# Three early loads outside the expert ring, ScalarE's loads moved to SyncE's queue, norm rows spread by matmuls, gates weighed later, last pair's loads in pieces

## The reference, cut to what matters

```python
x = layer_norm(DEEPNORM_ALPHA * x + mix, ln1_g, ln1_b)           # 256 tokens x 1024
logits = x @ router_w + router_b                                 # 32 experts
top_val, top_idx = top_k(logits, 4);  gates = softmax(top_val)
for each expert e and its tokens:
    gt = min(xb @ w_gate[e] + b_gate[e], 7)                      # w_gate, w_up, w_down: 1024 x 1024 f32 each
    up = clip(xb @ w_up[e] + b_up[e], -7, 7)
    ys = (gt * sigmoid(1.702 * gt) * (up + 1)) @ w_down[e] + b_down[e]
ffn[token] += gate * ys
x = layer_norm(DEEPNORM_ALPHA * x + ffn, ln2_g, ln2_b)
```

## Time and profile before

| | us |
|---|---|
| time, median of 3 runs | 2271.95 (2269.96 to 2273.84) |
| the profiled execution's own time | 2273.94 |
| its span, first to last instruction | 2272.1 |
| PE busy | 2092.2 (92%) |
| DVE busy | 837.5 (37%) |
| ACT busy | 583.3 (26%) |
| PE of the expert matmuls (L940) | 691.6 busy, 77.5 idle before them |
| DMA queue q1 (SP) | 589.54 MB |

### The profile page before, as it was taken

The page is one execution under the profiler, slowest core; times in us unless marked ns, Lnnn a source line. Parts: engine busy times, 40 slices in busy tenths (PEclk is TensorE's granted clock), DMA queues, the critical chain, the costliest instruction groups (busy, mean ns, idle before and its releaser), DMA issues.

```text
span 2272.1 us, 27092 instructions
## 1 busy us (share of the span) xinstructions
PE 2092.2 (92%) x11528; PEld 1397.2 (61%) x11528; DVE 837.5 (37%) x1507; ACT 583.3 (26%) x993; POOL 71.8 (3%) x119
## 2 busy tenths in 40 slices
PE   6988999999899988999999979899899999998887
PEld 3766888878687568999988933333334333433333
DVE  4353534352385546765456521111111121111112
ACT  3222423242242545544356310000000000000001
POOL 0000000000000330000031000000000000000000
PEclk8999999999999999999999989999999999999999
DMA  9543334233422554545532779999999999999996
GB/s 361 186 149 111 111 111 148 100 114 102 148 80 77 186 178 145 186 165 179 194 115 87 270 267 428 428 427 427 428 428 427 428 428 426 429 428 427 428 428 272
DMA packets 163040, 593.93 MB, mean 261 GB/s; under 512 B 10945, under 2 KB 83649, under 8 KB 137569
## 3 DMA queue, kind: packets, MB, share of 16 engines
q1 hardware_dynamic: 158848, 589.54, 65.7%
q10 hardware_dynamic: 4064, 2.58, 0.6%
HBM read 591.05 MB, written 1.05 MB: 261 GB/s over the span
## 4 chain that ended last, share of the span: by engine, by line
PE 74%; DMA 16%; DVE 5%; ACT 3%; issue 1%; ACTq 1%; SPq 1%; DVEq 0%
PE ps L940 21%; PE ps L283 14%; PE ps L284 13%; PE ps L285 13%; DMA ring<-in_w_up_dram 12%; DMA ring<-in_ada_w_dram 3%; PE ps L911 2%; PE ps L892 2%; DVE wr L1067 2%; PE ps L405 2%; ACT big L2012 1%; PE ps L419 1%; PE ps L413 1%; PE ps L720 1%; PE ps L965 0%
## 5 line engine op out<-in xcount | busy, mean ns | idle before, releaser
L940 PE MATMUL ps<-ring,big 128*64 128x512 f32 x3072 | 691.6, 606 | 77.5 <-DMA ring<-in_w_up_dram 50.5
L940 PEld LDWEIGHTS ps<-ring,big 128*64 128x64 f32 x3072 | 252.3, 139 | 489.5 <-issue 481.5
L283 PE MATMUL ps<-h_hi,wr 128*128 128x512 f32 (+1 forms) x960 | 341.6, 356 | 29.0 <-DVE h_lo L1119 24.7
L1067 DVE TENSOR_TENSOR wr<-ring,wr 128x1024 fp32r<-128x1024 f32 (+1 forms) x248 | 285.9, 1212 | 136.6 <-ACT wr L1712 136.5
L284 PE MATMUL ps<-h_lo,wr 128*128 128x512 f32 (+1 forms) x960 | 333.4, 347 | 0.0
L285 PE MATMUL ps<-h_hi,wr 128*128 128x512 f32 (+1 forms) x960 | 333.3, 347 | 0.0
L1712 ACT CAST wr<-ring 128x1024 fp32r<-128x1024 f32 (+1 forms) x248 | 238.8, 1033 | 126.3 <-PE ps L285 101.6
L283 PEld LDWEIGHTS ps<-h_hi,wr 128*128 128x128 f32 x960 | 185.4, 193 | 61.2 <-issue 34.4
L284 PEld LDWEIGHTS ps<-h_lo,wr 128*128 128x128 f32 x960 | 185.6, 193 | 23.4 <-issue 2.9
L285 PEld LDWEIGHTS ps<-h_hi,wr 128*128 128x128 f32 x960 | 185.1, 193 | 22.0
L2012 ACT ACTIVATE big<-ps,xT 128x128 f32<-128x128 f32 x64 | 24.1, 456 | 361.7 <-PE ps L892 361.7
(11 more groups left out here) (305 smaller groups left out, 2571.7 us busy)
## 6 DMA issues: line engine op xcount, KB each, us to landing
ring<-in_w_gate_dram SPq DMA_DIRECT2D x64, 2048.0 KB, 22.2
ring<-in_w_up_dram SPq DMA_DIRECT2D x62, 2048.0 KB, 18.4
ring<-in_w_down_dram SPq DMA_DIRECT2D x60, 2048.0 KB, 22.2
ring<-in_ada_w_dram SPq DMA_DIRECT2D x24, 2048.0 KB, 10.8
ring<-in_ffn_w_up_dram SPq DMA_DIRECT2D x44, 1024.0 KB, 7.6
ring<-in_ffn_w_down_dram SPq DMA_DIRECT2D x16, 1408.0 KB, 6.1
ring<-in_w_in_dram SPq DMA_DIRECT2D x9, 2048.0 KB, 8.0
ring<-in_odd_w_qkv_dram SPq DMA_DIRECT2D x6, 2048.0 KB, 8.1
```

What stands on the lines that cost most here:

```text
L283: e.matmul(o, l[0], r[0], start=first, stop=False)
L940: ins = e.matmul(pts[hf][HALF[z], :], lhs[:, k, HALF[z]], wt[:, k % 4, 512 * hf:512 * hf + 512], start=k == 0, stop=False, skip_group_chec ...
L1067: e.tensor_tensor(wr[:, x], ring[:, x], h.bitcast(F32), SUB).then_inc(s_wlo, 1)
```

## The change

- Loads 7, 8 and 9 (the second expert's last half of up, both experts' first half of down, of pair 0) go to twelve free pieces of SBUF outside the ring, in four DMAs each, with semaphores of their own (`EARLY`). 7 and 8 are issued behind load 2, once the merged rows are there; 9 behind load 6. The ring goes on with load 10 in slot 0 (`nth`).
- ACT issues none of the six DMAs. `b_down` and the two rows of the second norm (4 KB each, not spread) are issued by SP behind load 24. The sixteen small loads of `g8b8` are issued by SP one by one between the weight tiles of the second feed-forward part.
- The first norm's gain is spread by a matmul of ones with diagonal matrices, which DVE writes in pairs 2 and 7; the shift, times ALPHA, is added into the open banks in the same way, in place of a row in `GT`. The second norm's rows are spread by four matmuls, at pairs 7, 9, 11 and 13, and copied to SBUF by ACT.
- `select(0)` calls `gathered(0)` before `weigh`; the first pair's gates are turned at the end of pair 0, not before it; ACT's exponentials come behind `gathered(0)`.
- The last pair's gate k 4 to 7 and up k 0 to 3 come in pieces too. `last_scatter` starts with the half that DVE evacuates.

```diff
+    EARLY = {7: (big[:, 9088:10112], big[:, 10112:11136], big[:, 8064:9088], wkf[:, 0:1024]),
+             8: (big[:, 3072:4096], big[:, 4096:5120], big[:, 2048:3072], xT[:, 0:4, L:512]),
+             9: (xT[:, 4:8, L:512], wkf[:, 1024:2048], zz[:, :], big[:, 11136:12160])}
+    def nth(u):
+        return u if u < 7 else u - len(EARLY)
-    PIECES = [(LAST + 6, 0, 2), (LAST + 6, 2, 3), (LAST + 6, 3, 4), (LAST + 8, 0, 2), (LAST + 8, 2, 4),
+    PIECES = [(LAST + 2, 0, 2), (LAST + 2, 2, 4), (LAST + 4, 0, 2), (LAST + 4, 2, 4), (LAST + 6, 0, 2), (LAST + 6, 2, 3), (LAST + 6, 3, 4), (LAST + 8, 0, 2), (LAST + 8, 2, 4),
               (LAST + 10, 0, 2), (LAST + 10, 2, 3), (LAST + 10, 3, 4)]
...
         def last_scatter(b):
-            for n in range(2):
-                e.wait_ge(*emptied(("y", b, n)))
             for q in range(2):
                 for n in range(2):
+                    if q == 0:
+                        e.wait_ge(*emptied(("y", b, n)))
...
             both(pts, HT[turn_of(b)], u + 8, ("y", b, 0), emptied(("ht", b, 1)))
+            if b == 0:
+                turn_gates(0, U[1])
...
             if b in (4, 8):
-                e.wait_ge(s_rowg, 16)
-                e.matmul(pt[:, :], ones[0:1, :], grow[:, 512 * i:512 * i + 512], start=True,
-                         stop=True).then_inc(fullsem(("G", i)))
+                e.wait_ge(s_diag, 8 * i + 4)
+                e.matmul(pt[:, :], ones[:, :], dgG, start=True, stop=True).then_inc(fullsem(("G", i)))
             if b in (6, 10):
+                for n in range(2):
+                    e.matmul(ps[2 * n + i][:, :], ones[:, :], dgB, start=False, stop=False, skip_group_check=True)
...
+            if b in (7, 9, 11, 13):
+                pt = take(e, ("l2", i), bank=7)
+                e.matmul(pt[:, :], ones[0:1, :], l2row[i // 2][:, 512 * (i % 2):512 * (i % 2) + 512], start=True,
+                         stop=True).then_inc(fullsem(("l2", i)))
...
         gather(0, (6, 7))
-        turn_gates(0, 6)
...
             if b == 0:
+                gathered(0)
                 weigh()
...
+            if b in (2, 7):
+                for dg, x, by in ((dgG, "l1g", 1.0), (dgB, "l1b", ALPHA)):
+                    for c in range(4):
+                        e.tensor_scalar(dg[:, P * c:P * c + P], ident, col(x, 4 * i + c), by, MULT, MULT).then_inc(s_diag, 1)
...
-        e.dma_start(bdn[0:NE, :], a["b_down_2"]).then_inc(s_late2[0], 16)
-        e.wait_ge(s_blo, 2)
-        flat = a["cols"].rearrange("p c -> c p")
-        for row, sem_, c in ((grow, s_rowg, COLS["l1g"]), (bdn[NE:NE + 1, :], s_rowb, COLS["l1b"])):
-            e.dma_start(row.rearrange("o (c p) -> o c p", c=KC), flat[c:c + KC, :].unsqueeze(0),
-                        allow_slow_non_contiguous=True).then_inc(sem_, 16)
-        e.dma_start(l2g, a["ln2_2"][0:1, :].to_broadcast([P, D])).then_inc(s_late2[1], 16)
-        e.dma_start(l2b, a["ln2_2"][1:2, :].to_broadcast([P, D])).then_inc(s_late2[2], 16)
...
+            if b in (7, 9, 11, 13):
+                e.wait_ge(*filled(("l2", i)))
+                e.copy((l2g, l2b)[i // 2][:, 512 * (i % 2):512 * (i % 2) + 512], bank(("l2", i))[:, :]).then_inc(freesem(("l2", i)), 1)
...
         for t in range(W_O + 3, NW - 2):
             w(t)
+            i, c = divmod(t - W_O - 5, KC)
+            if 0 <= i < 2:
+                e.dma_start(g8b8[16 * c:16 * c + 16, 8 * i:8 * i + 8], g8[COLS[("l1g", "l1b")[i]] + c],
+                            allow_slow_non_contiguous=True).then_inc(s_g8, 16)
...
+            if u in EARLY:
+                for i, to in enumerate(EARLY[u]):
+                    rows_ = src[z].rearrange("(p k) n -> p k n", k=KC)[:, 4 * hf + i, :]
+                    e.dma_start(to, rows_ if len(to.shape) == 2 else rows_.rearrange("p (a b) -> p a b", b=L)).then_inc(
+                        s_early[u - 7], 16)
+                return
...
         expert(2)
+        e.wait_ge(*filled(("T2", 23)))
+        e.wait_ge(s_mlo, KC)
+        expert(7)
+        expert(8)
         e.wait_ge(*wlast[NW - 2])
         expert(3)
         expert(4)
         e.wait_ge(*wlast[NW - 1])
         expert(5)
         expert(6)
-        for u in range(7, 12 * (NE // 2)):
+        e.wait_ge(s_blo, 2)
+        e.wait_ge(*filled(("lgt", 1)))
+        expert(9)
+        for u in range(10, 12 * (NE // 2)):
             expert(u)
+            if u == 24:
+                e.dma_start(bdn, a["b_down_2"]).then_inc(s_late2[0], 16)
+                for i in range(2):
+                    e.dma_start(l2row[i], a["ln2_2"][i:i + 1, :]).then_inc(s_late2[1 + i], 16)
```

More of the change, by code:

```diff
@@ L174, in build @@
     s_alpha, s_xhat = sem("s_alpha"), sem("s_tail_normed")
-    s_piece = [sem(f"s_last_pair{i}") for i in range(8)]
+    s_piece = [sem(f"s_last_pair{i}") for i in range(12)]
+    s_early = [sem(f"s_early{i}") for i in range(3)]
     def cols_of(w, c0, n):
@@ L342, in landed_expert @@
     def landed_expert(u):
-        return s_w[u % 7], 16 * sum(x not in in_pieces for x in range(u % 7, u + 1, 7))
+        if u in EARLY:
+            return s_early[u - 7], 64
+        return s_w[nth(u) % 7], 16 * sum(x not in in_pieces and x not in EARLY and nth(x) % 7 == nth(u) % 7 for x in range(u + 1))
     def rows_used(kind, u):
@@ L938, in both @@
                     for z in range(2):
[L939 to L943, removed]
+                        if v + z not in EARLY:
+                            wt = view(ring, SLOT * XS[nth(v + z) % 7], 4, D)[:, k % 4, 512 * hf:512 * hf + 512]
+                        elif len(EARLY[v + z][k % 4].shape) == 3:
+                            wt = EARLY[v + z][k % 4][:, 2 * hf:2 * hf + 2, :]
+                        else:
+                            wt = EARLY[v + z][k % 4][:, 512 * hf:512 * hf + 512]
+                        ins = e.matmul(pts[hf][HALF[z], :], lhs[:, k, HALF[z]], wt, start=k == 0, stop=False,
+                                       skip_group_check=True)
+                        if k % 4 == 3 and hf == 1 and v + z not in EARLY:
+                            ins.then_inc(s_wused[nth(v + z) % 7])
                     if k == KC - 1 and hf == 0 and first:
@@ L979, in pair @@
             pts = [take(e, ("y", b, 0), bank=G[0]),
-                   take(e, ("y", b, 1), bank=G[1], by=(s_wused[last % 7], last // 7 + 1))]
+                   take(e, ("y", b, 1), bank=G[1], by=(s_wused[nth(last) % 7], nth(last) // 7 + 1))]
             e.wait_ge(*emptied(("ht", b, 0)))
             both(pts, HT[turn_of(b)], u + 8, ("y", b, 0), emptied(("ht", b, 1)))
+            if b == 0:
+                turn_gates(0, U[1])
             if nxt:
@@ L1612, in dve @@
         chosen(0)
[L1613 to L1615 removed]
+        e.tensor_scalar(alphaI, ident, ALPHA, None, MULT).then_inc(s_alpha, 1)
         for b in range(NE // 2):
@@ L1687, in dve @@
             aggr_at[n] = tail(e.bn_aggr(mv[n], bst[n]))
-        e.wait_ge(s_late2[1], 16)
-        e.wait_ge(s_late2[2], 16)
+        for i in range(4):
+            e.wait_ge(*emptied(("l2", i)))
         for n in range(2):
@@ L2036, in act @@
         gathered(0)
-        gates_turned(0)
+        e.wait_ge(s_gneg, 1)
+        for n in range(2):
+            ins = e.activation(ex4[:, n, :], top[:, n, 0:4], ACT.Exp, bias=top[:, n, 8:9], accum_out=top[:, n, 9:10])
+        ins.then_inc(s_gexp, 1)
         for b in range(NE // 2):
@@ L2215, in sync @@
         w(NW - 2)
-        for i, x in enumerate(("l1g", "l1b")):
-            src = a["cols"].rearrange("(b k) c -> c b k", k=KC)
-            for c in range(KC):
-                e.dma_start(g8b8[16 * c:16 * c + 16, 8 * i:8 * i + 8], src[COLS[x] + c],
-                            allow_slow_non_contiguous=True).then_inc(s_g8, 16)
         e.wait_ge(*emptied(("S2", 23)))
```

48 lines of the change are left out of this document (27 added, 21 removed).

## The result

The changed kernel took 2254.76 us (median of 5, 2254.24 to 2259.89) against 2273.05 for the kernel before (median of 5, 2269.96 to 2273.84): a ratio of 0.993, 95% interval 0.9915 to 0.9945, so 18.3 us faster. The prediction was 2251.8 with a range of 2246 to 2263.

The account below looks back on a forecast made before the run. The expert loop was taken as bound by its loads; -18.0 + 0.3 - 2.1 + 0.45 - 0.75 = -20.1 us on the profiled 2273.94 gave 2253.8, or 2251.8 from the median, range 2246 to 2263.

Parts of the forecast that it names:

- Part 1: Start: with gathering before weighing and no loads issued on ACT, pair 0 starts at 1321.2 instead of 1329.26, gate 13.95 us.
- B: Stretch, router's last group to pair 0: -8.06 us. As rival: PE starts pair 0 no earlier, 2262.4 us, 10%.
- Part 2: Expert loop: three early loads save 14.8 us, a 7.1 us stall eats half; transfers end 18.0 us earlier.
- the lead: Expert loop: time from PE's last use of a ring slot until its next load begins, taken as 4.3 us.
- Part 3: Moved loads: 0.3 us for those now inside the bound stretch, zero for the sixteen small loads (bounds -1 and +3).
- Part 4: Last pair: gate and up in pieces gain 2.1 us, less 0.45 for the pieces' price.
- D: Stretch, last down's end to span's end: -0.75 us. As rival: nothing measurable moves, 2268 to 2272 us, 4%.
- The 0.4 us to spare: Last pair's down: it reaches k 7 at 2253.4, after the last transfer at 2253.0, so the 2.1 is kept.
- The price of pieces: Last pair: pieces move at 418 GB/s instead of 427, 2% of four more loads, 0.45 us.
- Part 5: End: two of the last scatter's eight instructions run under ACT's copy, -0.75 us.
- A: Rival, expert loop: slots come free in time without a stall, transfers end 25.1 us earlier, 2244.7 us, 6%.
- C: Stretch, pair 0 to last down's end: -11.28 us. As rival: PE becomes the bound, clock falls, 2284 us, 4%.

Follow-up runs that it names:

- the repeat: The changed kernel run again with no edit; 2257.21 us (2255.07 to 2259.21), ratio 0.9933.

## Why the prediction was right, and the step that failed

**Part 1** held: ScalarE's queue was what held pair 0, the gather was what it came down to, and gate took 13.95. -9.3 instead of -8.06 because the gather itself took 5.44 and not 6.62; with a long gather it is -8.1. That the gather was short is luck: it comes with when the clock rose, which no edit sorts. Of the two things that part 1 joins, the loads on ScalarE were the cause (moved away alone, B shrank by 8.2), and the order of evacuating and weighing was not (undone, pair 0 still followed the gather at once).

**Part 2** held in place and size. Relative to pair 0's start the pause was forecast from 45.7 to 52.8 us and lies at about 43 to 49.5; the transfers were forecast to end 914.55 after it (2235.0, and the 0.75 of parts 3 and 4, less 1321.2) and ended 914.9 after it (2233.3, share 0.23 in 2232 to 2234, then only 0.03). There was no second pause. That the early loads make the pause was shown by leaving them out (+7.6). Two sizes under it were off and cancel: the lead from a slot's last use to transfers was taken as 4.3 us, but pair 0 ends at 1366.89 and the transfers restart at 1367.8, 0.9 later; and with 175 loads from there to 2233.3 a load takes 4.95, not 4.92. The lead was counted back over eleven loads, which puts every loss at the loop's start into it. In the kernel before, too, the transfers were back at 1339.7, 0.9 behind the issue of load 7 (share 0.00 in 1338.8 to 1339.7, 1.14 in the microsecond after it); where in the eleven loads the rest was lost was not tried. Both ends of the pause move with the lead, its length does not. One sign failed: no wait for loads was forecast in pairs 0 to 2, and there is one in pair 2:

```profile
1445.28 8.78 PE L959 MATMUL ps<-ring,big 128*64 128x512 f32 x32 [2.62 <-DMA ring<-in_w_up_dram]
```

**Part 3** held: no cost of the small loads in SP's queue in either place. What it missed lies in "the two spread rows and the gathered rows lay in the gap and paid nothing to the loop": true in the gap, but with the old loads moved out of it the expert loads started 4.2 us late, beside the spread rows. The 0.3 us of the loads behind load 24 was not tried by itself.

**Part 4.** Predicted a net 1.65; undone, it costs 3.2 to 3.5 at down's end, and 1.7 to 2.1 with D (against either profile of the changed kernel). Against the kernel before the pieces brought less: down ended 4.3 us behind the last transfer there and 2.9 here, 1.4 of the 2.1. Most of the rest of the 3.5 is the wait inside up of the run without them (15.65), which the kernel before (13.95) did not have; why it has one is open. The 0.4 us to spare at the last piece were there (it landed at 2233.88, and its first instruction began at 2234.25). What the sum lacked is that down took 14.32, not 13.95: the wait stands at the 33rd of its 64 instructions, for the first piece of its second half, as in the row above with the count read early and in the repeat:

```profile
2230.04 7.09 PE L959 MATMUL ps<-ring,big 128*64 128x512 f32 x32 [0.23 <-DMA ring<-in_w_down_dram]
```

The price of pieces that was taken from the 418 GB/s row did not show: the transfers end 914.9 us behind pair 0 with four pieces more and 915.0 without them. So here the rule of the Trainium skill (DMA: Bandwidth & Descriptors, Specifications), line rate from 512 B up, stands closer to the runs than the value taken, though 2207 to 2227 shows 418 GB/s again.

**Part 5** is the step that failed: "L921 starting within 0.2 us of down's end" and -0.75 became a start 2.18 behind it and +1.23. The order was worth 0.8 to 0.9 where nothing else held the chain (the pair of runs with both jumps gone). In this kernel it was held by the jump over unused blocks, which the prediction put at nothing. The earlier trace rows could not show it: there the scatter waited for ACT, and the jump's time, 2.6 us behind a packet at 2255.5, ran out under down and that wait. That the scatter is held by the jump is shown by the run that puts it ahead of the blocks. That the jump shows only now because down ends 2.3 us behind the landing of the last piece, and not 3.8, fits all traces but was not tried by itself.

**Rivals.** A (no stall) fails by the 0.01 in 1362 to 1366; B by pair 0's start; C by a clock of 0.98 in 1380 to 2207, the same as before; D by the time.

The sum: 20.1 forecast, 18.3 measured. The step that accounts for it is part 5 (2.0 of D); B's extra 1.2, which is luck, and C's missing 1.05 (0.4 of it transfers that end later, 0.7 part 4) nearly cancel.

## What to carry to other kernels

Loads taken out of a ring free transfers but no slots: work out which slot comes back last, and subtract the pause that a full ring then makes. An engine that issues loads with many single elements, or rows spread to 128 partitions, should not be one on which a chain waits, and moving such loads beside bulk loads brings part of the cost along (of the 8.2 us won at the start here, 4.3 were left at the end); build the rows by matmul. When the last wait before a branch goes, look at what the branch itself takes, and put the usual case in front of the rare one; it was worth 1.5 us of D here, less than whole times can show.

## What was not expected of the hardware

- Behind a jump over skipped code the first instruction started 2.5 to 2.9 us after a 16 KB packet on the instruction queue, on TensorE, and VectorE showed an idle time of 3.14 put down to "issue" in the same place; the run that keeps the usual case ahead of the code on both engines has neither.
- A pause of TensorE of this size can cost more than itself. In two runs (gates weighed first; small loads back) it was 2.43 and 2.49 us, the granted clock then fell to 0.58 and 0.68, towards the lower level of 1.2 GHz, and the eight scatter instructions took 5.37 us instead of 3.67, so that D was 18.0 and 18.1. Stretches of the run with the gates weighed first, the pause and the scatter:

```profile
2235.90:2238.32 2.42, 0.00 (x1) 0.03 (x1) 0.00 (x0) 1.75 (x2) 0.00 (x0) 1.00 0.02 7
2238.32:2240.82 2.50, 2.50 (x4) 1.14 (x5) 0.00 (x0) 0.12 (x1) 0.00 (x0) 0.58 0.04 10
```

  In the changed kernel's traces the pause was 2.18 and 2.26, and without the early loads 2.34, and the scatter took 3.67. In the loop the wait of 2.62 shown above was followed by 32 instructions in 8.78 us instead of 7.09, at a clock of 0.61 in 1445.28 to 1449.
- The same gather took 5.2 to 5.5 us in five traces of the changed kernel and its variants and 6.6 to 6.7 in six, by when the granted clock rose in it. No edit sorts the traces so: runs that differ only at the kernel's end fall in both groups.
